# Second block: where the convolution's taps, the layer norm's steps, the rotations and the last modulation rows stand

## The reference, cut to what matters

```
for l in range(2):
    mod  = silu(c) @ w_ada[l] + b_ada[l]          # 9 x 1024 numbers: shifts, scales, gates
    modc = silu(c_ctx) @ w_ada[l] + b_ada[l]
    h = h + 0.5 * gt1 * swiglu(ada_norm(h, g1, sh1, sc1), w1, w3, w2)   # width 2816
    u = ada_norm(h, g_mix, sh2, sc2)
    z_conv, z_cq, z_ckv, z_kr, z_four = split(u @ w_in)
    # attention of 8 heads: q from cq, k and v from ckv, 32 rotated dimensions in q and k
    k, v = mla_kv(z_ckv, z_kr, ...);  q = mla_q(z_cq, ...)     # apply_rope inside
    attn = softmax(q k^T * scale) v
    # convolution: 384 channels, 31 taps, then a layer norm over the channels
    v = a * sigmoid(gt);  v = conv31(v) + b;  v = silu(layer_norm(v)) @ w_pw + b_pw
    four = real(fft2(z_four)) @ w_fourier + b_f
    g0, g1, g2 = split(sigmoid(u @ w_bg + b_bg))
    h = h + gt2 * ((g0 * conv + g1 * (attn @ w_o) + g2 * four) @ w_out)
    h = h + 0.5 * gt3 * swiglu(ada_norm(h, g2, sh3, sc3), w1, w3, w2)
# the context tokens run through the same steps; in layer 1 only their keys and values are needed
```

## Time and profile before

| | us |
|---|---|
| median of 3 runs (lowest, highest) | 2822.07 (2813.7, 2827.72) |
| the profiled execution | 2823.88 |
| its span, first to last instruction | 2822.1 |
| PE busy | 2644.0 (94% of the span) |
| DVE busy | 1724.8 (61%) |
| ACT busy | 1046.6 (37%) |
| POOL busy | 135.6 (5%) |

### The profile page before, as it was taken

One profiled execution on the slowest core, in us unless ns is written; L12 is line 12 of the kernel. 1 busy time (PEld: TensorE's weight loads), 2 busy tenths in 40 slices (PEclk: granted clock), 3 DMA queues, 4 the chain that ended last, 5 costly groups with the idle time before them and its releaser, 6 DMA issues.

```text
span 2822.1 us, 37400 instructions
## 1 busy us (share of the span) xinstructions
PE 2644.0 (94%) x15172; PEld 2280.8 (81%) x15172; DVE 1724.8 (61%) x2714; ACT 1046.6 (37%) x1575; POOL 135.6 (5%) x105
## 2 busy tenths in 40 slices
PE   7998879899799998998999999998999989898998
PEld 7998659899688887766878788887888877698898
DVE  5767474576676656455665666656555455586654
ACT  5445422444422223333243422223222224345543
POOL 0000013000000000032010000000000000310000
PEclk9999879899899999999999999999999999999999
DMA  7764200376355544211223255544343333154554
GB/s 239 233 226 177 75 1 1 124 237 221 113 177 181 174 148 139 72 34 54 93 84 103 91 185 174 173 155 132 120 145 129 125 116 97 49 158 149 164 186 144
DMA packets 110108, 380.90 MB, mean 135 GB/s; under 512 B 12016, under 2 KB 17392, under 8 KB 109552
## 3 DMA queue, kind: packets, MB, share of 16 engines
q1 hardware_dynamic: 108928, 373.32, 41.0%
q10 hardware_dynamic: 1008, 5.18, 0.5%
HBM read 377.40 MB, written 1.05 MB: 134 GB/s over the span
## 4 chain that ended last, share of the span: by engine, by line
PE 88%; DVE 7%; ACT 3%; issue 1%; POOL 0%; DMA 0%; SPq 0%; DVEq 0%; ACTq 0%
PE B L1195 25%; PE B L1196 25%; PE B L1197 25%; PE B L1411 2%; PE B L1210 1%; DVE w_lo L1717 1%; PE B L1211 1%; PE B L1212 1%; PE B L1427 1%; ACT w_hi L1480 1%; PE B L1335 1%; PE B L1321 1%; PE B L1328 1%; PE B L1418 1%; DVE TMP L1741 0%
## 5 line engine op out<-in xcount | busy, mean ns | idle before, releaser
L1195 PE MATMUL B<-U,w_hi 128*128 128x256 f32 (+1 forms) x2896 | 965.3, 333 | 13.1 <-DVE w_lo L1717 9.3
L1196 PE MATMUL B<-U,w_hi 128*128 128x256 f32 (+1 forms) x2896 | 957.9, 331 | 0.0
L1197 PE MATMUL B<-U,w_lo 128*128 128x256 f32 (+1 forms) x2896 | 957.8, 331 | 0.0
L1717 DVE TENSOR_TENSOR w_lo<-w_raw,w_hi 128x1024 fp32r<-128x1024 f32 (+3 forms) x587 | 683.9, 1175 | 438.7 <-ACT w_hi L1480 437.9
L1480 ACT ACTIVATE w_hi<-w_raw 128x1024 fp32r<-128x1024 f32 (+3 forms) x587 | 591.8, 1012 | 552.2 <-PE B L1197 527.0
L1195 PEld LDWEIGHTS B<-U,w_hi 128*128 128x128 f32 x2896 | 550.0, 190 | 70.6 <-issue 16.0
L1196 PEld LDWEIGHTS B<-U,w_hi 128*128 128x128 f32 x2896 | 548.1, 189 | 54.8 <-issue 2.1
L1197 PEld LDWEIGHTS B<-U,w_lo 128*128 128x128 f32 x2896 | 548.0, 189 | 52.8
L1195 PE MATMUL B<-HHf,w_hi 128*128 128x256 f32 (+1 forms) x1056 | 352.0, 333 | 0.0
L1196 PE MATMUL B<-HLf,w_hi 128*128 128x256 f32 (+1 forms) x1056 | 352.0, 333 | 0.0
L1197 PE MATMUL B<-HHf,w_lo 128*128 128x256 f32 (+1 forms) x1056 | 352.0, 333 | 0.0
(11 more groups left out here) (319 smaller groups left out, 2541.2 us busy)
## 6 DMA issues: line engine op xcount, KB each, us to landing
w_raw<-in_w SPq DMA_DIRECT2D x504, 512.0 KB, 4.2
w_ada<-in_w SPq DMA_DIRECT2D x144, 512.0 KB, 3.5
w_raw<-in_w SPq DMA_DIRECT2D x58, 384.0 KB, 3.2
w_raw<-in_w SPq DMA_DIRECT2D x16, 240.0 KB, 2.6
X<-in_x SPq DMA_DIRECT2D x2, 1024.0 KB, 9.7
w_raw<-in_w SPq DMA_DIRECT2D x8, 256.0 KB, 3.1
BW<-in_bias ACTq DMA_DIRECT2D x1, 1536.0 KB, 10.3
K<-in_consts ACTq DMA_DIRECT2D x2, 640.0 KB, 4.1
```

The lines of the kernel that those rows point to most:

```text
L1195: pe.matmul(o, hi, xh, start=i == 0, stop=False)
L1196: pe.matmul(o, hi, xl, start=False, stop=False)
L1197: e = pe.matmul(o, lo, xh, start=False, stop=i == last)
L1717: dve.tensor_tensor(w_lo[:, plan.slot[u], 0:n], w_raw[:, plan.ring[u], 0:n], w_hi[:, plan.slot[u], 0:n].bitcast(F32), ALU.subtract).then_i ...
```

## The change

Four things change. The taps' pace becomes 4 halves a turn in layer 0 (2 taps) and 7 in layer 1 (3 or 4 taps). `share` divides by one place less and is capped, so the last modulation row of a part stands at its last place but one. The layer norm's steps get more `yield`s between them. `rope` gets a `yield` behind it, so a head's scores stand in the turn after its rotation.

```diff
-TAPS, LATE, WIDTH, WIDTH1 = (3, 4), 4, 8, 6
+TAPS, LATE, WIDTH, WIDTH1 = (4, 7), 4, 8, 6
...
     def ffn(self, p, n, wts, need, gate, old):
-        turns, share = 0, lambda i: i * ADA[p] // (NF + 7)
+        turns, share = 0, lambda i: min(i * ADA[p] // (NF + 6), ADA[p])
         junk = self.TM.take(5, 6)
...
             self.add("ln_sum", key=l, n=n, t=t)
             yield
+            yield
             self.add("ln_mean", key=l, n=n, t=t, b=b)
             TM.done(t, ("ln_mm", l))
+            yield
             yield from TM.room(2)
             stat = Stat(self, f"ln{l}", n)
...
             PS.done(b, ("ln_cen", (l, 2)))
             yield
+            yield
+            yield
             rb = stat.rsqrt(384, ring=TM)
             yield
             for c in range(3):
                 self.add("ln_out", key=(l, c), n=n, rb=rb, need=(old,))
+                yield
...
                 rope((l, h), q, n)
+                yield
                 todo[h] = ns
                 prepared[h] = (q, kk)
```

## The result

The changed kernel takes 2807.61 us in the median of 22 runs (2799.6 to 2815.5), the kernel before 2817.43 in 22 runs (2807.9 to 2827.9) on the same chips. The ratio is 0.9957, with a 95% interval of 0.9946 to 0.9969: 12 us gained (9 to 15), where the prediction said 30. The time lies inside the predicted range (2775 to 2815), but the sum was wrong by 18 us.

A forecast was written before the change was run, and what follows sets the result against it. PE, busy 94% of the span, was taken as the bound, leaving its waits and half-clock stretches to mend. Modulation -8.4, rotation -11.8, layer norm -8.7, clock -11.4, POOL +8.3, taps +2 gave -30.0 us: 2792 us, range 2775 to 2815.

The forecast's parts named there:

- the sum: Whole kernel: gains of 8.4, 11.8, 8.7 and 11.4 us against losses of 8.3 and 2, together -30.0 us.
- A clock that falls behind waits: Two mixing parts: half-clock stretches behind the waits should go where the waits go, 11.4 us gained, bounds 0 and 14.8.

The follow-up runs named there:

- e3: The changed kernel with the turn behind the rotation kept in layer 1 alone, taken out in layer 0; ratio to the kernel before 0.9947.
- e4: The changed kernel with 3 and 4 taps in every two turns, as before, in place of 4 and 7; ratio to the kernel before 0.9957.
- e10: The kernel before with the turn behind the rotation and 4 and 7 taps in every two turns, no layer norm turns; one execution of 2813.57 us.
- e6: The kernel before with GpSimd dividing only the first quarter of each row of the attention's weights; one execution of 2818.55 us.
- e9: The kernel before with the layer norm's turns and nothing else; ratio to the kernel before 1.0018.
- e11: The changed kernel with the Fourier product free to start once the rotation is issued, and the layer norm's three outputs in one turn again; ratio to the kernel before 0.9898.
- e13: The kernel before with the modulation's edit, the rotation's turn and the Fourier product free from the rotation's issue; no layer norm turns, 3 and 4 taps; ratio 0.9922.
- e1: The kernel before with the modulation's end a tile sooner and nothing else of the change; ratio to the kernel before 0.9982.

## What to carry to other kernels

A clock that falls behind waits is a term of its own: work it out from the waits that will be there afterwards, the new ones too, and not from those that go. A line that moves one piece of work apart from another also moves what stood between them: here one `yield` took a 24-matmul product away from ahead of the transposes, and letting that product start a turn sooner turned 12 us of gain into 35. Profile one order twice before laying a few microseconds to an edit: the same order gave 134.0 us three times in one place, and 141.3 and 144.0 in another. Test an edit that looks harmless by itself and with the others: in layer 0's mixing part the rotation's turn alone changed 470.0 us to 469.7, the other edits alone to 465.6 (e3), and both together to 475.8.

## What the runs showed of the hardware

- Matmuls of 256 columns follow each other at 113.3 or at 117.8 ns at a granted clock of 0.99, and the level can hold for a whole feed-forward part. The last part takes 182.2 to 183.6 us in twelve profiles and 189.7 to 190.0 in three (before, e4, e10), with the same instructions. The second part of the first block does the same: 202.6 to 203.8 us in eleven profiles and 209.5 to 210.7, at 117.8 ns, in e6, e9, e11 and e13; in e9 the first part is slow too. I found nothing in the traces that sets it.
- The first block ends at 729.4 to 744.3 us, again with the same code but for the modulation's 2 us. Its mixing part makes up to 9 us of that (316.7 to 325.8), the pitch of the matmuls the rest. Together with the 7 us of the last part this is about the spread of the runs (2807.9 to 2827.9). With it, a single profile of a kernel tells stretches, and only the ratio of many runs tells the total.
- The granted clock is not a function of the order of the instructions. With the same order on four engines, half-clock time was 13.7 and 20.5 us in the heads of layer 0 (e10, after), and the granted clock 0.89 and 0.94 in the heads of layer 1 (before, e1).
- Waits of 9.3 to 11.7 us in one stretch went with anything from 3.4 to 20.5 us of half clock. Half of that came on top of the waits' own length: 1.7 us at least and 10.2 at most.
